# Modulation products with the condition rows stationary on four column groups

## The chip, the cores and the metric

One core of one Trainium2 chip runs one program. The time is that of the device for one execution, in microseconds (us), the median of several runs. TensorE (PE in the profile, with its weight loads as PEld), VectorE (DVE), ScalarE (ACT), GpSimd (POOL) and SyncE (SP) each work through a stream of instructions of their own and wait for each other through semaphores. SyncE, GpSimd and ScalarE also issue the transfers between memory and SBUF. In this kernel GpSimd does almost nothing else.

## The reference

One step of a two-layer decoder, for a prompt of 1,024 rows and eight sample sequences of four rows, 1,056 rows in all, model width 1,024, float32. The first layer is gated linear attention, the second differential attention, which reads keys and values made in between. Each of the three norms is modulated by a condition vector `c`, one for the prompt and one for each sample, nine rows:

```
def ada_mod(x, c, g, w_ada, b_ada, n):
    mod = jax.nn.silu(c) @ w_ada + b_ada
    parts = [p[:, None, :] for p in jnp.split(mod, n, axis=-1)]
    h = rms_norm(x, g) * (1.0 + parts[1]) + parts[0]
    return h, parts[2:]
```

`parts[2:]` are the gates on the output projections. Three weights are used, `ada_w_a` (1024 x 3072, first norm and first gate), `ada_w_kv` (1024 x 2048) and `ada_w_b` (1024 x 3072). In tiles of 128 columns, that is 24 + 16 + 24 = 64 tiles, each a product of a 1024 x 128 block with nine vectors.

## The kernel before

Everything is held transposed, the features on the partitions. The program has stages that end in a barrier: `setup`, `gla` (four heads), an output projection, `attention` (eight heads), an output projection. The tile `mod` (128 x 64 x 9) holds the modulation, a tile of 128 features in each of 64 places, `M_A` = 0, `M_KV` = 24, `M_B` = 40. `cT` holds silu(c), transposed.

`setup` turns x into `B2` (TensorE transposes, L281, VectorE copies, L367), stores it to memory (L336), makes the first norm (squares on ScalarE L136, sums on VectorE L143, a sum over partitions by `pe_sum` L148, `act_rstd`, then `dve_rstd` L161, which multiplies x in place and so waits for the store), and applies the modulation on ScalarE (`act_affine`, L169), with the low part of a high and low split on VectorE (L406). All 24 tiles of `ada_w_a` are made here, in three groups of four quarters: `cT` is stationary, 256 columns of the weights move (L301), into rows of nine partitions, which are copied (L384), turned (L309) and placed (L388). A fourth of a group is 1 MB; SyncE loads two of the four buffers and GpSimd two.

`gla` runs the same body for each head `i`. TensorE's order in a head is written out by hand: keys (units 3 to 5), the gate, z (units 9 to 14), the modulation products `modulate(0)` and `modulate(1)`, the value projection `project_v`, then a loop over eight chunks `t`, each with `levels(t + 1)` (L626), for t up to 4 another `project_v`, `output(t)` (L637, L639), for t = 1 to 6 one `modulate`, and `update(t + 1)` (L647). Behind the loop stand the products of the eight sample states (L701), `modulate(8)`, the update of the sample states (L708), `modulate(9)`, the next head's query projection and the sums of squares (L719). Each result goes to one of the two banks of `psP`; the n-th result of a head is `unit` n, counted in `s_proj` when summed and in `s_pfree` when copied out, so that a bank waits for the copy of the unit two before.

A modulation product (L649 to L654) makes one tile of 128: for each of eight `k`, the 128x128 block of weights is stationary and the nine columns of `cT[:, k, :]` move. ScalarE places it with the bias (L770). The 40 tiles of `ada_w_kv` and `ada_w_b` are made so, ten a head. GpSimd loads each tile's weights, 512 KB, into one of two buffers `wm` as soon as the product two before is done (L559).

In the chunk loop VectorE masks the eight level products (L921), reduces them (L926, into `Am`, which `output(t)` needs), and updates the state (L933); in chunk 5 it also makes the low part of the next head's first weights (L855), for which ScalarE must have made the high part (L740) behind the copy of that chunk's output (L826). The state of the samples, `sst`, 1 MB, has a tile of its own and is loaded by SyncE at the head's start (L516) and stored at its end (L520); behind that store stands the store of `Gs` (L526), for which VectorE waits at the end of the head (L957).

## Time and profile before

| | |
|---|---|
| runs | 1987.09, 1981.51, 1983.03 us; median 1983.03 |
| span of the profiled execution | 1985.5 us (its own time is not given apart) |
| TensorE busy | 1825.2 us (92%) |
| VectorE, ScalarE busy | 716.8 us (36%), 707.4 us (36%) |
| GpSimd busy | 234.2 us (12%), transfers issued |
| mean granted TensorE clock | 0.908 of 2.4 GHz |
| memory | 158.03 MB moved, mean 80 GB/s |

A busy share is an average over stages; what a stage is worth is read from that stage. An idle stretch of an engine is shown in brackets with what ended it. float32 products show as two records each. The granted clock is 1.00 or 0.50 in any short stretch, that is 2.4 or 1.2 GHz.

### The profile page before, as it was taken

To read this page: it belongs to the slowest core of one execution; us is meant where nothing else is said; L and a number is where in the kernel's file an instruction comes from. 1 tells how busy PE (TensorE), PEld (TensorE's weight loads), DVE (VectorE), ACT (ScalarE), POOL (GpSimd) and SP (SyncE) were. 2 spreads that over 40 slices of the span, in tenths; PEclk is the share of its full clock that TensorE was granted. 3 is DMA by queue.
4 is the path that set the end of the run, shared out by engine and by line. 5 is a ranking of instruction groups with operands and counts; after the bars stand their busy time and mean duration, and the time that the engine had idled before them with its cause. 6 is when DMAs were issued, how large, how long until landed. Compare 5 with 4: busy or idle time off the path is not lost. (4 is left out here: it accounts for less than half of the span.)

```text
span 1985.5 us, 32185 instructions
## 1 busy us (share of the span) xinstructions
PE 1825.2 (92%) x10195; PEld 1469.0 (74%) x10195; DVE 716.8 (36%) x1296; ACT 707.4 (36%) x1241; POOL 234.2 (12%) x372
## 2 busy tenths in 40 slices
PE   6899999999999969879998999989999899998798
PEld 3499889889889959746675776757767576665698
DVE  4536347327427533323215132141221412314321
ACT  2433143134125131254245343443434434344411
POOL 0011001100100100022030120311202112030000
PEclk8999799879878959989899898998999989999799
DMA  8622231231221242333022220222202222021143
GB/s 304 195 65 55 66 118 54 67 116 46 77 86 54 67 140 87 119 99 98 23 66 61 65 83 20 67 62 64 84 19 67 63 63 85 19 69 52 33 119 87
DMA packets 129119, 158.03 MB, mean 80 GB/s; under 512 B 13331, under 2 KB 103986, under 8 KB 129051
## 3 DMA queue, kind: packets, MB, share of 16 engines
q0 software_dynamic: 23776, 73.46, 12.6%
q1 hardware_dynamic: 94330, 70.61, 11.6%
q10 hardware_dynamic: 10944, 12.98, 1.9%
q8 instruction: 52, 0.85, 0.2%
q14 instruction: 17, 0.13, 0.0%
HBM read 127.41 MB, written 29.59 MB: 79 GB/s over the span
## 5 line engine op out<-in xcount | busy, mean ns | idle before, releaser
L1341 PE MATMUL at_psP<-B,w 128*128 128x352 f32 x768 | 253.4, 489 | 16.1 <-ACTq L1488 16.1
L1341 PEld LDWEIGHTS at_psP<-B,w 128*128 128x128 f32 x768 | 154.2, 203 | 102.6 <-issue 31.4
L1326 POOL DMA_DIRECT2D at_vc<-in_cache_v x256 | 139.0, 543 | 275.0 <-issue 275.0
L1065 PE MATMUL op_ps<-op_G_high,op_w_high 128*128 128x352 f32 x384 | 126.3, 329 | 30.4 <-DVE op_G_low L1135 25.6
L574 PE MATMUL gl_psP<-Hh,gl_w_high 128*128 128x352 f32 x384 | 131.9, 344 | 3.3 <-ACT gl_qT L757 1.7
L1350 PE MATMUL at_psP<-w,B 128*128 128x128 f32 (+1 forms) x1152 | 132.4, 275 | 0.0
L1350 PEld LDWEIGHTS at_psP<-w,B 128*128 128x128 f32 (+1 forms) x1152 | 129.6, 183 | 2.7
L574 PE MATMUL gl_psP<-Hl,gl_w_high 128*128 128x352 f32 x384 | 129.0, 336 | 0.0
L574 PE MATMUL gl_psP<-Hh,gl_w_low 128*128 128x352 f32 x384 | 128.5, 335 | 0.0
L1065 PE MATMUL op_ps<-op_G_low,op_w_high 128*128 128x352 f32 x384 | 124.5, 324 | 0.0
L1065 PE MATMUL op_ps<-op_G_high,op_w_low 128*128 128x352 f32 x384 | 124.5, 324 | 0.0
L1651 DVE CUSTOM_DVE_ANT_0 at_S<-at_psS,at_bias 128x256 f32<-128x256 f32 (+7 forms) x128 | 92.2, 754 | 79.2 <-PE at_psS L1377 78.8
L1341 PE MATMUL at_psP<-B,at_w_z 128*128 128x352 f32 x384 | 114.9, 459 | 0.0
L1395 PE MATMUL at_psO<-at_wT,at_v 128*128 128x128 f32 x576 | 83.9, 295 | 25.1 <-ACT G L1554 25.1
L1686 DVE SCALAR_TENSOR_TENSOR G<-G,at_subg,at_rs 128x1056 f32 x8 | 10.6, 1319 | 256.8 <-ACT at_rs L1600 256.8
L1341 PEld LDWEIGHTS at_psP<-B,at_w_z 128*128 128x128 f32 x384 | 73.0, 190 | 40.6
L1395 PEld LDWEIGHTS at_psO<-at_wT,at_v 128*128 128x128 f32 x576 | 76.5, 207 | 31.8 <-issue 29.2
L1065 PEld LDWEIGHTS op_ps<-op_G_high,op_w_high 128*128 128x128 f32 x384 | 73.4, 191 | 32.6 <-DVE op_G_low L1135 27.2
L1541 ACT ACTIVATE at_S<-at_S,at_nmx 128x256 f32<-128x256 f32 (+7 forms) x128 | 97.3, 763 | 0.0
L653 PEld LDWEIGHTS gl_psP<-cT,gl_wm 128*128 128x128 f32 x640 | 93.4, 232 | 2.9 <-issue 2.6
L653 PE MATMUL gl_psP<-cT,gl_wm 128*128 128x9 f32 x640 | 93.3, 284 | 0.0
L1377 PE MATMUL at_psS<-at_kT,at_qT 64*128 64x512 f32 (+3 forms) x384 | 85.4, 528 | 5.6 <-ACT at_ko L1534 5.4
(252 smaller groups left out, 3342.9 us busy)
## 6 DMA issues: line engine op xcount, KB each, us to landing
at_kc<-in_cache_k SPq DMA_DIRECT2D x256, 64.0 KB, 1.9
at_vc<-in_cache_v POOLq DMA_DIRECT2D x256, 64.0 KB, 2.2
w<-in_w_in_a POOLq DMA_DIRECT2D x24, 512.0 KB, 5.5
gl_wm<-in_ada_w_b POOLq DMA_DIRECT2D x24, 512.0 KB, 4.6
gl_wm<-in_ada_w_kv POOLq DMA_DIRECT2D x16, 512.0 KB, 6.0
su_w<-in_ada_w_a POOLq DMA_DIRECT2D x6, 1024.0 KB, 8.8
su_w<-in_ada_w_a SPq DMA_DIRECT2D x6, 1024.0 KB, 9.9
scr_xT<-B ACTq DMA_DIRECT2D x1, 4224.0 KB, 14.6
```

What stands on the lines that cost most here:

```text
L574: mm = nc.tensor.matmul(out, stationary(a, k), moving(b, k), start=(k == 0 and n == 0), stop=(k == KC - 1 and n == 2))
L653: mm = nc.tensor.matmul(psP[:, b, 0:NC], wm[:, n % MS, k, :], K["cT"][:, k, :], start=(k == 0), stop=(k == KC - 1))
L1065: mm = nc.tensor.matmul(ps[:, u % 2, 0:THIRD], ws[:, b, k, :], thirds(gs[:, k, :])[j], start=(k == 0 and n == 0), stop=(k == KC - 1 and n ...
L1326: pool.dma_start(vc[:, bass.ds(n, 1), :], A["cache_v"][bass.ds(page, 1), :, bass.ds(i, 1), :].rearrange("n p h d -> p (n h) d")).then_inc( ...
L1341: mm = nc.tensor.matmul(psP[:, unit % 2, 0:THIRD], w[name][:, k, :], thirds(src[:, k, :])[unit % 3], start=(k == 0), stop=(k == KC - 1))
L1350: mm = nc.tensor.matmul(psP[0:n, (9 + r) % 2, (t - lo) * P:(t - lo + 1) * P], hk[:, k, t * P:t * P + n], w["v"][:, k, :], start=(k == 0), ...
L1377: mm = nc.tensor.matmul(psS[:, 2 * comp + lo // 512, 0:hi - lo], qT[rows, t * P:(t + 1) * P], kT[rows, lo:hi], start=True, stop=True)
L1395: mm = nc.tensor.matmul(psO[:, (t % 2) * P:(t % 2 + 1) * P], v[:, k, :], wT[:, t % 2, k * P:(k + 1) * P], start=(k == 0), stop=(k == t))
L1541: A_(s, s, ACT.Exp, scale=-1.0, bias=nmx[:, t % 2, comp:comp + 1], accum_out=rsum[:, t % 2, comp:comp + 1]).then_inc(s_exp, 1)
L1651: V.tensor_tensor_reduce(S[:, t % 2, comp, 0:n], psS[:, 2 * comp:2 * comp + 2, :].rearrange("p a k -> p (a k)")[:, 0:n], bias[:, TP - n:TP ...
L1686: V.scalar_tensor_tensor(g, g, subg[:, 0:1], rs[:], ALU.mult, ALU.mult).then_inc(s_g1, 1)
```

## The change

The condition rows become the stationary operand everywhere, padded from nine to 32 columns with zeros (`CW`), and the weights move. The output is then 32 partitions high, and four such products stand in the four column groups of the array, each with its own quarter of the weight's columns (`CG` = 4).

In `setup` only the first 2,048 columns of `ada_w_a` are multiplied, which the first norm needs: eight loads of 128 rows x 2,048 columns (1 MB each, four buffers), for each one four multiplications of 512 columns. The sum for the norm comes after the fourth. The result, 128 partitions x 512, is copied, turned by four full transposes and placed. `xt` has five buffers instead of three, and the weight loads begin when the fifth x tile is there.

In `gla`, each head makes twelve tiles (48 in all, the rest of `ada_w_a` among them) in four products `modulate(0)` to `modulate(3)`. Each takes two blocks of 128 rows of a weight, 1,536 columns wide (`MW` = 384 in each column group), and VectorE adds them up in `macc` (`keep_mods`). In chunk 4 `turn_mods` turns the sum with three transposes and VectorE places it (`place_mods`). A load of both `wm` buffers waits for the product before. The two products ahead of the value projection stay where they were; two stand in chunks 1 and 2, and none behind that. ScalarE has no part in it any more. The count of freed banks is kept apart for each bank (`s_pf`). The sample state moves into rows of `B2` that the level products use, so its load waits for the last of them (`s_lv`), and VectorE waits for its store at the end of the head. GpSimd's loop over heads is unrolled.

```diff
+CG = 4
+CW = 32
...
+            K["cT"] = sb("cT", [P, KC, CW], c)
...
-        XB = 3
+        XB = 5
         xt = tile("xt", [P, XB, D])
-        mrow = tile("mrow", [NC, 2, 512])
-        w = tile("w", [P, 4, KC, 256])
+        mrow = tile("mrow", [P, 512])
+        w = tile("w", [P, 4, CG * 512])
...
-        def load_mod(eng, slots):
-
-            wd = A["ada_w_a"].rearrange("(k p) n -> p k n", p=P)
-            with eng.Fori(0, GROUPS) as i:
-                for j in slots:
-                    eng.wait_ge(s_wfree, i * 4 + j + 1)
-                    apart(eng, passed[slots[0]])
-                    eng.dma_start(w[:, j], wd[:, :, bass.ds(i * 1024 + 256 * j, 256)]).then_inc(s_w[j], 16)
-
-        passed = {0: K["sem"]("passed_sp"), 1: K["sem"]("passed_pool"), "pe": K["sem"]("passed_pe")}
+        def load_mod(eng, first):
+
+            for k in range(first, KC, 2):
+                if k >= 4:
+                    eng.wait_ge(s_wfree, k - 3)
+                else:
+                    eng.wait_ge(s_x[XB - 1], 16)
+                eng.dma_start(w[:, k % 4], A["ada_w_a"][k * P:(k + 1) * P, 0:CG * 512]).then_inc(s_w[k % 4], 16)
...
+                nc.gpsimd.memset(cT[:], 0.0).then_inc(s_set, 1)
+                load_mod(pool, 1)
...
-                def modulations(i):
-                    for j in range(4):
-                        pe.wait_ge(s_w[j], (i + 1) * 16)
-                        for k in range(KC):
-                            mm = nc.tensor.matmul(psM[0:NC, j // 2, (j % 2) * 256:(j % 2 + 1) * 256], cT[:, k, :], w[:, j, k, :],
-                                                  start=(k == 0), stop=(k == KC - 1))
-                        mm.then_inc(s_wfree, 1)
-                    for b in range(2):
-                        pe.wait_ge(s_mrow, 2 * i + b + 1)
-                        pe.wait_ge(s_mev, 2 * i + b + 1)
-                        apart(pe, passed["pe"])
-                        for m in range(4):
-                            mm = nc.tensor.transpose(psT[:, b, m * NC:(m + 1) * NC], mrow[:, b, m * P:(m + 1) * P], ident[0:NC, 0:NC])
-                        mm.then_inc(s_mT, 1)
-
-                modulations(0)
-                norm.pe_sum(pe)
-                with pe.Fori(1, GROUPS) as i:
-                    modulations(i)
+                for k in range(KC):
+                    pe.wait_ge(s_w[k % 4], 16 * (k // 4 + 1))
+                    for j in range(CG):
+                        mm = nc.tensor.matmul(psM[32 * j:32 * j + 32, 0, :], cT[:, k, :], w[:, k % 4, 512 * j:512 * (j + 1)], start=(k == 0), stop=(k == KC - 1))
+                    mm.then_inc(s_wfree, 1)
+                    if k == 3:
+                        norm.pe_sum(pe)
+                pe.wait_ge(s_mrow, 1)
+                for m in range(4):
+                    mm = nc.tensor.transpose(psT[:, 0, m * P:(m + 1) * P], mrow[:, m * P:(m + 1) * P], ident[:])
+                mm.then_inc(s_mT, 1)
...
-                dve.sem_inc(s_mev, 2)
-
-                def modulations(i):
-
-                    for b in range(2):
-                        dve.wait_ge(s_wfree, i * 4 + 2 * b + 6)
-                        nc.vector.tensor_copy(mrow[:, b, :], psM[0:NC, b, :]).then_inc(s_mrow, 1)
-                    for b in range(2):
-                        dve.wait_ge(s_mT, 2 * i + b + 1)
-                        at = i * 8 + 4 * b
-                        nc.vector.tensor_tensor(mod[:, bass.ds(at, 4), :], psT[:, b, 0:4 * NC].rearrange("p (m c) -> p m c", c=NC),
-                                                bcast(vec[:, bass.ds(at, 4)].unsqueeze(2), P, 4, NC), ALU.add).then_inc(s_mev, 1)
-
-                modulations(0)
                 dve.wait_ge(s_out, 16)
                 norm.dve_rstd(dve)
-                modulations(1)
-                dve.wait_ge(s_mev, 2 + 4)
+                dve.wait_ge(s_wfree, KC)
+                nc.vector.tensor_copy(mrow[:], psM[:, 0, :]).then_inc(s_mrow, 1)
+                dve.wait_ge(s_mT, 1)
+                nc.vector.tensor_tensor(mod[:, M_A:M_A + 16, :].rearrange("p (j m) c -> p j m c", j=CG),
+                                        psT[:, 0, :].rearrange("p (m j x) -> p j m x", j=CG, x=CW)[:, :, :, 0:NC],
+                                        bcast(vec[:, M_A:M_A + 16].rearrange("p (j m) -> p j m", j=CG).unsqueeze(3), P, CG, 4, NC), ALU.add).then_inc(s_mev, 1)
+                dve.wait_ge(s_mev, 1)
...
-    MODS, MS = 10, 2
+    MODS, MS, MW = 4, 2, 384
...
-        wm = tile("wm", [P, MS, KC, P])
-        sst = tile("sst", [P, SB, DV])
+        wm = tile("wm", [P, MS, CG * MW])
+        macc = tile("macc", [P, MW])
...
+        sst = X[:, 5:7, :].rearrange("p a t -> p (a t)")[:, 0:SB * DV].rearrange("p (b d) -> p b d", b=SB)
...
+        def freed(eng, i, unit):
+
+            eng.wait_ge(s_pf[unit % 2], i * (UNITS // 2) + (unit // 2 + 2))
...
-        V_UNITS = {(0, 2): 17, (2, 4): 18, (4, 5): 19, (5, 6): 20, (6, 7): 22, (7, 8): 24, (8, 9): 26}
-        M_UNITS = [15, 16, 21, 23, 25, 27, 28, 29, 30, 31]
-        M_CHUNK = [[], [2], [3], [4], [5], [6], [7], [], [8, 9]]
-        UNITS = 32
+        V_UNITS = {(0, 2): 17, (2, 4): 18, (4, 5): 19, (5, 6): 20, (6, 7): 22, (7, 8): 24, (8, 9): 25}
+        M_UNITS = [15, 16, 21, 23]
+        T_UNITS = [26, 27]
+        M_CHUNK = [[], [2], [3], [], [], [], [], [], []]
+        UNITS = 28
...
+                    sp.wait_ge(s_lv, CH * (i + 1))
+                    apart(sp, passed["sp"])
                     sp.dma_start(sst[:], A["state_gla"][:, bass.ds(i, 1), :, :].rearrange("b h k v -> k (b h) v")).then_inc(s_sin, 16)
...
+                    parts = [(wa, 2 * D, wkv, 0), (wkv, 512, wkv, 512 + D), (wb, 0, wb, D), (wb, D + 512, wb, 2 * D + 512)][i]
                     for n in range(MODS):
 
-                        pool.wait_ge(s_proj, i * UNITS + (UNITS + M_UNITS[n - MS] if n >= MS else M_UNITS[n - MS]) + 1)
-                        apart(pool, passed["pool"])
-                        src = wkv[:, :, bass.ds(i * 4 * P + n * P, P)] if n < 4 else wb[:, :, bass.ds(i * 6 * P + (n - 4) * P, P)]
-                        pool.dma_start(wm[:, n % MS], src).then_inc(s_wm[n % MS], 16)
-                        if n == 3 and not last:
+                        pool.wait_ge(s_proj, i * UNITS + (UNITS + M_UNITS[n - 1] if n else M_UNITS[MODS - 1]) + 1)
+                        for kk in range(MS):
+                            rows = slice((MS * n + kk) * P, (MS * n + kk + 1) * P)
+                            pool.dma_start(wm[:, kk, 0:D], parts[0][rows, parts[1]:parts[1] + D]).then_inc(s_wm[kk], 16)
+                            pool.dma_start(wm[:, kk, D:D + 512], parts[2][rows, parts[3]:parts[3] + 512]).then_inc(s_wm[kk], 16)
+                        if n == 1 and not last:
...
                     def modulate(n):
-                        pe.wait_ge(s_wm[n % MS], 16 * (MODS // MS * i + n // MS + 1))
                         b = bank(i, M_UNITS[n])
-                        for k in range(KC):
-                            mm = nc.tensor.matmul(psP[:, b, 0:NC], wm[:, n % MS, k, :], K["cT"][:, k, :], start=(k == 0), stop=(k == KC - 1))
+                        for kk in range(MS):
+                            pe.wait_ge(s_wm[kk], 32 * MODS * i + 32 * (n + 1))
+                            for j in range(CG):
+                                mm = nc.tensor.matmul(psP[32 * j:32 * j + 32, b, 0:MW], K["cT"][:, MS * n + kk, :], wm[:, kk, MW * j:MW * (j + 1)],
+                                                      start=(kk == 0), stop=(kk == MS - 1))
                         mm.then_inc(s_proj, 1)
+
+                    def turn_mods():
+                        freed(pe, i, M_UNITS[MODS - 1])
+                        for u, subs in zip(T_UNITS, ((0, 1), (2,))):
+                            b = bank(i, u)
+                            for m in subs:
+                                mm = nc.tensor.transpose(psP[:, b, (m % 2) * P:(m % 2 + 1) * P], macc[:, m * P:(m + 1) * P], ident[:])
+                            mm.then_inc(s_proj, 1)
...
                         output(t)
                         for n in M_CHUNK[t]:
                             modulate(n)
+                        if t == 4:
+                            turn_mods()
                         if t + 1 < NT:
...
-                    modulate(NT)
                     pe.wait_ge(s_khm, i + 1)
                     pe.wait_ge(s_lm, CH * i + CH)
                     for b in range(SB):
                         mm = nc.tensor.matmul(psL[:, b // 2, (b % 2) * DV:(b % 2 + 1) * DV], khm[:, b, :], v[0:TS, NT, :], start=True, stop=True)
                     mm.then_inc(s_ups, 1)
-                    modulate(NT + 1)
...
-                    def modulation(n):
-                        b = done(i, M_UNITS[n])
-                        apart(act, passed["act"])
-                        A_(mod[:, bass.ds(mod_tile(i, n), 1), :].rearrange("p a c -> p (a c)"), psP[:, b, 0:NC], ACT.Identity,
-                           bias=vec[:, bass.ds(mod_tile(i, n), 1)]).then_inc(s_pfree, 1)
+                        act.sem_inc(s_pf[b], 1)
...
+                    def keep_mods(n):
+
+                        unit = M_UNITS[n]
+                        dve.wait_ge(s_proj, (i + 1) * UNITS + unit + 1)
+                        if n:
+                            freed(dve, i, M_UNITS[n - 1])
+                            V.tensor_tensor(macc[:], macc[:], psP[:, unit % 2, 0:MW], ALU.add).then_inc(s_pf[unit % 2], 1)
+                        else:
+                            V.tensor_copy(macc[:], psP[:, unit % 2, 0:MW]).then_inc(s_pf[unit % 2], 1)
+
+                    def place_mods():
+
+                        tiles = bass.ds(i * M_HEAD + M_FIRST, M_HEAD)
+                        for u, lo, n in zip(T_UNITS, (0, 2), (2, 1)):
+                            dve.wait_ge(s_proj, (i + 1) * UNITS + u + 1)
+                            apart(dve, passed["dve"])
+                            V.tensor_tensor(mod[:, tiles, :].rearrange("p (j m) c -> p j m c", j=CG)[:, :, lo:lo + n, :],
+                                            psP[:, u % 2, 0:n * P].rearrange("p (m j x) -> p j m x", j=CG, x=CW)[:, :, :, 0:NC],
+                                            bcast(vec[:, tiles].rearrange("p (j m) -> p j m", j=CG)[:, :, lo:lo + n].unsqueeze(3), P, CG, n, NC),
+                                            ALU.add).then_inc(s_pf[u % 2], 1)
...
+                        if L >= 5:
+                            keep_mods(L - 5)
...
+                        if t in (1, 2):
+                            keep_mods(t + 1)
+                        if t == 4:
+                            place_mods()
...
+                    dve.wait_ge(s_sout, 16 * (i + 1))
```

## Rows read from the trace of the kernel before

**Rows 1.** The page's busy times: TensorE and its weight loads, the others.

```profile
PE 1825.2 (92%) x10195; PEld 1469.0 (74%) x10195; DVE 716.8 (36%) x1296; ACT 707.4 (36%) x1241; POOL 234.2 (12%) x372
```

**Rows 2.** Windows view, instructions on `gl_wm` alone: PE, PEld, POOL busy, PEclk, DMA share, GB/s.

```profile
100.00:720.00 620.00, 93.31 (x640) 93.37 (x640) 37.02 (x40) 0.87 0.25 73
```

**Rows 3.** Timeline of TensorE in head 1: start, length in us, instruction, idle before.

```profile
309.11 3.63 PE L653 MATMUL gl_psP<-cT,gl_wm 128*128 128x9 f32 x32
...
340.82 1.85 PE L653 MATMUL gl_psP<-cT,gl_wm 128*128 128x9 f32 x16
...
376.67 0.49 PE L637 MATMUL gl_psO<-gl_Am,gl_v 128*128 128x128 f32 x2 [3.60 <-DVE gl_Am L926]
...
377.82 3.42 PE L653 MATMUL gl_psP<-cT,gl_wm 128*128 128x9 f32 x16
...
382.69 0.80 PE L637 MATMUL gl_psO<-gl_Am,gl_v 128*128 128x128 f32 x2
...
385.46 1.92 PE L701 MATMUL gl_psO<-gl_ec,gl_sst 128*128 128x4 f32 x16 [0.85 <-ACT B L826]
...
391.66 3.58 PE L653 MATMUL gl_psP<-cT,gl_wm 128*128 128x9 f32 x16
```

**Rows 4.** Timeline of VectorE and GpSimd in head 1.

```profile
311.78 0.88 POOL L559 DMA_DIRECT2D gl_wm<-in_ada_w_kv  x1 [24.06 <-PE gl_psP L653]
...
313.70 1.32 DVE L900 TENSOR_TENSOR gl_gk<-B 128x1024 f32<-128x1024 f32 x2
...
325.23 1.26 DVE L916 TENSOR_TENSOR gl_gk<-gl_gk,gl_kT 128x1056 f32<-128x1056 f32 x1
...
372.36 1.23 DVE L855 TENSOR_TENSOR gl_w_low<-w,gl_w_high 128x1024 fp32r<-128x1024 f32 x1 [5.45 <-ACT gl_w_high L740]
373.50 1.22 DVE L921 TENSOR_TENSOR gl_tmp<-gl_psL,gl_masks 128x1024 f32<-128x1024 f32 x1
374.75 1.87 DVE L926 TENSOR_REDUCE gl_Am<-gl_tmp 128x128 f32<-128x1024 f32 x1
```

**Rows 5.** Windows: PE, PEld, DVE, ACT, POOL busy, PEclk, DMA share, GB/s.

```profile
32.00:67.00 35.00, 33.67 (x153) 14.43 (x154) 22.04 (x27) 13.45 (x13) 3.91 (x5) 0.95 0.98 336
...
312.70:316.00 3.30, 3.30 (x17) 3.30 (x17) 3.27 (x9) 3.01 (x4) 2.32 (x3) 0.50 0.73 176
...
377.50:384.30 6.80, 6.80 (x34) 6.08 (x34) 4.43 (x6) 0.65 (x2) 1.77 (x2) 0.50 0.11 12
...
387.70:411.60 23.90, 23.90 (x87) 21.82 (x87) 4.45 (x9) 3.61 (x5) 0.39 (x1) 0.50 0.14 46
```

**Rows 6.** Timeline of TensorE, an attention head: L1377 two row groups, L1408 full height.

```profile
1054.09 1.13 PE L1377 MATMUL at_psS<-at_kT,at_qT 64*128 64x512 f32 x4
...
1056.58 1.07 PE L1408 MATMUL at_psP<-at_ko,at_QZ 128*64 128x512 f32 x2
...
1073.37 2.04 PE L1377 MATMUL at_psS<-at_kT,at_qT 64*128 64x512 f32 x8
```

**Rows 7.** DMA issues: count, KB each, median us from issue to landing.

```profile
gl_wm<-in_ada_w_b POOLq DMA_DIRECT2D x24, 512.0 KB, 4.6
...
scr_xT<-B ACTq DMA_DIRECT2D x1, 4224.0 KB, 14.6
...
gl_sst<-in_state_gla SPq DMA_DIRECT2D x4, 1024.0 KB, 7.1
out_state_s<-gl_sst SPq DMA_DIRECT2D x4, 1024.0 KB, 4.4
```

**Rows 8.** Timeline of the setup: TensorE, VectorE, ScalarE.

```profile
50.93 14.08 PE L301 MATMUL su_psM<-su_w,cT 128*9 128x256 f32 x64
...
54.67 9.44 DVE L161 TENSOR_TENSOR B<-B,su_rs 128x1056 f32<-128x1056 f32 x8 [5.42 <-ACT su_rs L156]
...
66.79 1.24 ACT L169 ACTIVATE Hh<-B,mod 128x1024 fp32r<-128x1024 f32 x1 [12.22 <-DVE mod L397]
```

**Rows 9.** Timeline of TensorE at the end of head 3.

```profile
712.81 6.79 PE L719 MATMUL gl_psL<-B,ones 128*128 128x352 f32 x12 [2.29 <-ACT B L834]
```

More of the change, by code:

```diff
@@ L284, in _ @@
                         pe.wait_ge(s_tab, 16 * TABS)
-                        nc.tensor.transpose(psM[:, 0, 0:V_N], rows[:], ident[0:V_N, 0:V_N]).then_inc(s_vecT, 1)
+                        nc.tensor.transpose(psM[:, 0, 0:V_N], rows[:], ident[0:V_N, 0:V_N]).then_inc(s_turn, 1)
                         pe.wait_ge(s_csil, 1)
@@ L288, in _ @@
                             mm = nc.tensor.transpose(psM[:, 1, k * NC:(k + 1) * NC], crow[:, k * P:(k + 1) * P], ident[0:NC, 0:NC])
-                        mm.then_inc(s_cps, 1)
+                        mm.then_inc(s_turn, 1)
                 pe.wait_ge(s_lsum, 2)
                 pe.wait_ge(s_vec, 1)
-                nc.tensor.matmul(psM[:, 0, 0:2], ones[0:1, :], lams[0:1, :], start=True, stop=True).then_inc(s_lps, 1)
+                nc.tensor.matmul(psM[:, 0, 0:2], ones[0:1, :], lams[0:1, :], start=True, stop=True).then_inc(s_turn, 1)
                 pe.wait_ge(s_xev, 2 * (NT + 1))
@@ L406, in low @@
                     nc.vector.tensor_tensor(K["Hl"][:, k, :], xT[:, k, :], K["Hh"][:, k, :], ALU.subtract).then_inc(s_lo, 1)
-                for k in range(KC - 2):
-                    low(k)
-                modulations(2)
-                for k in range(KC - 2, KC):
+                for k in range(KC):
                     low(k)
 def gla(nc, A, OUT, SCR, K):
-    MODS, MS = 10, 2
+    MODS, MS, MW = 4, 2, 384
     with ExitStack() as c:
@@ L472, in gla @@
         s_lowps, s_low = sem("low_summed"), sem("low_ready")
-        s_proj, s_pfree = sem("proj_summed"), sem("proj_bank_free")
+        s_proj, s_pf = sem("proj_summed"), [sem(f"proj_bank_free{b}") for b in range(2)]
         s_v = sem("v_ready")
@@ L565, in _ @@
                 load_g2(0)
-                over_heads(pool, head)
+                for i in range(HA):
+                    head(i, i == HA - 1)
             @block.tensor
@@ L781, in head @@
                     for j in range(3):
-                        A_(thirds(kT[:])[j], psP[:, done(i, 3 + j), 0:THIRD], ACT.Copy).then_inc(s_pfree, 1)
+                        A_(thirds(kT[:])[j], psP[:, done(i, 3 + j), 0:THIRD], ACT.Copy).then_inc(s_pf[(3 + j) % 2], 1)
                     high(i, Z_TILE + 1, 5)
@@ L826, in head @@
                         A_(Gs[:, :, t * P:t * P + n], psO[:, 0:2 * n].rearrange("p (a t) -> p a t", a=2), ACT.Copy).then_inc(s_oev, 1)
-                        for m in M_CHUNK[t]:
-                            modulation(m)
                         if t == 5 and not last:
```

54 lines of the change are left out of this document (25 added, 29 removed).

## The prediction

> **What bounds the kernel now.** I began with the page's busy times [rows 1]: TensorE is busy 92% of the span, VectorE and ScalarE each about a third. So time on TensorE's own instruction stream is what counts, until a wait appears in it. Next the windows view of the instructions that touch the weight buffer `gl_wm` [rows 2]: the 40 modulation products of the four heads hold TensorE for 93.3 us, and the weight loads are in progress for as long. Each product is eight loads of a full 128x128 block for nine moving columns. Then the timeline of head 1 [rows 3], where the reader is to see three places. Two products stand back to back ahead of the value projection (3.63 us). Six stand in the loop over chunks, of which five take 1.85 us and the sixth, behind a 3.60 us idle, 3.42 us. Two stand in the tail, 3.58 us each (one row stands for both), with no idle between the sample products and the next head's query projection. The timeline of the other engines in the same head [rows 4] says what ends the 3.60 us idle: VectorE's reduction, which stood behind a weight split that waited for ScalarE. The windows by clock [rows 5] show that the short products are also where the clock is lost: 1.2 GHz (0.50) from 312.7 to 316.0 behind two of them, again from 377.5, and through the 23.9 us of the tail.
>
> **The new product.** Per head: four products instead of ten, each of eight multiplications of 384 moving columns, in four column groups. The old setup products give the serial price: 32 multiplications of 256 columns took 14.08 us [rows 8], 0.44 us each, so 0.66 us for 384 columns and 5.2 us for a product. Do the four column groups run at the same time? No row shows column groups. The nearest rows are the attention scores, which lie in two row groups [rows 6]: one full-height multiplication of 512 columns takes 1.07 us, two half-height ones 1.13 us, four 2.04 us. Two groups run at once, at no cost per group. If four column groups do the same, a product is two steps of 0.66 us and 0.2 us of drain, 1.5 us. Bounds: 1.5 and 5.2 us; I take 1.5, since the groups seen behave that way.
> The Trainium skill, page "TensorE: Matmul & The Clock Gate", section "Part 3: Packing small matmuls", gives a measured 2.38 times for three column tiles of 32 at 512 columns; by it, as an estimate, a product would cost 1.6 us. The same section says that a weight load overlaps matmuls in flight only where the row group differs, and here all four groups share their rows; by that the product would be serial or worse. The trace does not bear this out for full blocks: loads and products of one row group fill the same 93 us [rows 2].
>
> **Ahead of the value projection.** Before, products 0 and 1 each had their own buffer, loaded long ahead. Now one product uses both buffers (two blocks of 128 rows), and its load waits for the end of the product before. Products 0 and 1 are still back to back in TensorE's stream. So product 1 waits for a whole load: two blocks of 0.75 MB, four DMA issues on GpSimd's queue. An issue took 0.88 us for a transfer in 1,024 pieces [rows 4]; with 256 pieces I take 0.6. A 0.5 MB weight transfer lands 4.6 us after its issue [rows 7]. First block: 0.4 (release) + 0.6 + 4.4 = 5.4 us behind product 0; second about 1.8 us later; then its 0.75 us of product. The value projection starts at 309.1 + 1.5 + 7.2 + 0.75 = 318.5 instead of 312.6: +5.9 us (4 to 9). The idle costs clock too, where 3.3 us at half clock are paid already [rows 5]: +0.8. Queued behind product 1: the value projection on TensorE; on VectorE, the copy of product 1 stands before the k-hat differences and the level multiplications, 11.5 us from 313.70 to 325.23 [rows 4], which meet the 13.0 us of projection up to the first level product; they stay hidden by about 1 us. Together +6.7 us a head.
>
> **In the chunk loop.** Products 2 and 3 gain 0.35 us each; product 3's load has the 6.2 us between them, so 0.3 us of wait. Products 4 to 6 (old numbering) leave, 1.85 each, and three transposes come, 0.6 us. What this frees meets VectorE: it now waits in order for the products (0.5 us to add each) and for the transposes in chunk 4, before it may mask chunk 5. From the transposes on the chain is VectorE's: placing 0.5, mask and reduce 3.2 us [rows 4], against 2.3 us of update and levels on TensorE, so chunk 5's output waits 1.4 us. Then 0.9 us of output, 1.5 of ScalarE's copy and split, the low part 1.2, mask and reduce 3.2, chunk 6's output. In head 1's old times the transposes end at 362.9 and that output moves from 376.67 to about 373.3; chunk 7's, which had the 3.42 us product ahead, moves from 382.69 to 376.9, VectorE's state update, mask and reduce behind it.
>
> **The sample state.** It moves into rows that the levels use, so its 1 MB load is issued only when the last level product is done (375.8 in the same times: 373.3, 1.4 of output, 0.6 of update, 0.5), not half a head ahead. It took 7.1 us when it shared the engines with a store of G, which it no longer does; a 1 MB store alone took 4.4 [rows 7]. I take 5.7 with 0.3 for SyncE: the sample products start at 381.8 instead of 385.46, 3.7 us earlier, where without this wait they would start at 379.5. So 2.3 us of it is exposed. The wait for the state's store before the next head costs nothing: the store of G is issued behind it on the same queue, and VectorE waits for that already.
>
> **The tail.** Two products leave: -7.2 us. ScalarE no longer waits for them, so squares and sums follow sooner. The query projection behind runs at half clock now; with denser work ahead it may run at full, and against that the sample products stay at half longer. I take -1.0 (-3 to +1.5). Heads 0 to 2: 6.7 - 3.7 - 7.2 - 1.0 = -5.2 us each, -15.6. In head 3 there is no split in chunk 5 and no 3.60 us idle: its chunk loop gives back only about 0.3. But the sums wait for ScalarE's squares behind the last product until 712.81 [rows 9]; they then follow the last state update, 6.1 us sooner. Head 3: 6.7 - 0.3 - 6.1 = +0.3 us.
>
> **The setup.** The products shrink from 96 of 256 columns to 32 of 512, and the weights from 12 MB to 8. The end is set elsewhere: the x rows, squares, the sum over partitions, the scaling of 9.44 us from 54.67, then ScalarE's affine from 66.79 [rows 8]. Five x tiles now come first, the weights behind them, and the small tables share the engines with less, so I take x as turned some 4 us sooner (1 to 6). The sum no longer waits for products, but the scaling waits for the store of x to memory, 4.3 MB, which took 14.6 us with little beside it [rows 7]. Now 4.2 MB of weights go beside it: both at the 336 GB/s of this stretch [rows 5] are 25 us, from about 27.8 to 53, so the scaling starts at 53 instead of 54.67. The copy, four transposes and the addition stand behind it, 2 us, where before 2.7 us did. I take -3 us (-8 to +1).
>
> **Sum.** -15.6 + 0.3 - 3 = -18.3 us against the profiled execution. The page gives only its span, 1985.5 us, which lies 2.5 above the median of the runs; I take what lies around it as unchanged and subtract from the median: 1983.0 - 18.3 = 1964.7, 1965 us.
>
> **Rivals.** *Serial column groups* (ends on the other side). A product costs 5.2 us: product 0 and 1 add 6.4 more a head, products 2 and 3 7.4 more; VectorE's slack gives back some 2. About +11.8 a head on the forecast, +47 in all; in the setup the store hides it: 2012 us. Place: every product in the heads. It decides from about 2.9 us a product on, where the total crosses zero. For it: no row has column groups. Against: [rows 6]. By the Trainium skill's rule on loads, quoted above, it would be this case. *The waits cost clock.* Each head gets two idles that it did not have, 5 and 2 us, and the row behind the 3.60 us idle is 6.8 us of half clock [rows 5]. If each idle brings as much, the value projection loses 3 us more than now and the tail gains nothing: some +3.5 a head, 1979 us. *Cheaper all round*: the loads land in 4 us and the query projection runs at full clock: -3 a head more, the setup -8: 1948 us. *The change does not do what it says* has no place here: the instructions are fixed.
>
> **Chances.** Forecast 0.60 (own range 1950 to 1972), clock 0.17, serial 0.15, cheaper 0.08. Range: down to 1944 for the cheap case; upward it takes in the clock case with the upper load bound, 1990, and leaves out the serial one. A measurement of this kernel tells 0.3%, 6 us, from no change. Faster: forecast, cheap and a third of the clock case, 0.73; same: 0.11; slower: serial and a tail, 0.16.
>
> **What would show it.** In the profile after: the products' line near 4 x 1.5 us a head and four starts a few tens of ns apart (serial: 0.66 us apart); an idle of about 5 us inside product 1, ended by a DMA into `gl_wm`; 1 to 2 us of idle before the sample products ended by the DMA into the state; chunk 5's output waiting for VectorE; the affine at about 64 us. The prediction is wrong if product 1's idle is over 9 us, if VectorE's levels end after the value projection, or if half clock spreads into the projections.

## The result and the profile after

The changed kernel takes 1989.35 us (median of 5 runs, 1988.21 to 1990.97); beside it the kernel before took 1983.03 us (1981.51 to 1987.09). The ratio is 1.0032, 95% interval 1.0019 to 1.0045: about 0.3% slower, where 1965 us was predicted. The time lies just inside the range, by its upper end.

The profiled executions hide the difference: spans of 1985.5 and 1986.4 us. A further trace of each (runs below) explains that. Executions lie some 2 us above their spans, so the profiled one of before took 1987.09 us, its slowest run; the second trace of that kernel has a span of 1978.4 us, the second of the changed kernel 1991.6 us. So stages are compared here as means of two traces each. By these the work behind the four heads begins at 732.6 us before and at 739.6 us after, and the rest is equal. The loss of 7.0 us is all in setup and heads.

The page's busy times of the changed kernel (compare [rows 1]), then the windows view of the instructions on `gl_wm` ([rows 2]; PE, PEld, POOL, clock, DMA share, GB/s):

```profile
PE 1739.4 (88%) x9675; PEld 1374.7 (69%) x9675; DVE 720.1 (36%) x1310; ACT 696.9 (35%) x1201; POOL 229.1 (12%) x395
```

```profile
100.00:720.00 620.00, 30.85 (x256) 6.22 (x256) 35.46 (x64) 0.87 0.25 80
```

TensorE lost 86 us of busy time, 62 of them in the head products, and the kernel gained nothing: idle time stands in the place of the work. The waits of TensorE in the heads say which (total us, times, longest; a wait of 21.1 us ahead of head 0 is left out):

```profile
PE gl_psO L627 <- DVE gl_Am L942: 20.0, 11, 3.6
PE gl_psP L644 <- DMA gl_wm<-in_ada_w_kv: 16.8, 6, 7.9
PE gl_psO L703 <- DMA B<-in_state_gla: 15.1, 4, 4.6
PE gl_psP L644 <- DMA gl_wm<-in_ada_w_b: 12.4, 5, 5.2
```

Three of the four rows are transfers, 44.3 us, and no such row stands among the waits of the kernel before. Its row for the reduction into `gl_Am` is the first one's counterpart, and that has grown by 9.2 us, in chunk 5 above all:

```profile
PE gl_psO L637 <- DVE gl_Am L926: 10.8, 3, 3.6
```

The timeline of TensorE in head 1 shows their places (compare [rows 3]):

```profile
311.54 1.50 PE L644 MATMUL gl_psP<-gl_wm,cT 128*32 128x384 f32 x16
320.94 1.50 PE L644 MATMUL gl_psP<-gl_wm,cT 128*32 128x384 f32 x8 [7.90 <-DMA gl_wm<-in_ada_w_kv]
323.00 1.51 PE L644 MATMUL gl_psP<-gl_wm,cT 128*32 128x384 f32 x8 [0.56 <-DMA gl_wm<-in_ada_w_kv]
...
362.49 0.85 PE L644 MATMUL gl_psP<-gl_wm,cT 128*32 128x384 f32 x8 [0.80 <-DMA gl_wm<-in_ada_w_kv]
...
379.71 0.49 PE L627 MATMUL gl_psO<-gl_Am,gl_v 128*128 128x128 f32 x2 [1.77 <-DVE gl_Am L942]
...
386.68 0.61 PE L627 MATMUL gl_psO<-gl_Am,gl_v 128*128 128x128 f32 x2 [3.59 <-DVE gl_Am L942]
...
395.98 3.54 PE L703 MATMUL gl_psO<-gl_ec,B 128*128 128x4 f32 x16 [4.61 <-DMA B<-in_state_gla]
...
400.01 3.58 PE L703 MATMUL gl_psO<-gl_ec,B 128*128 128x4 f32 x16
```

Product 0 takes 1.50 us. Product 1 waits 7.90 us for its first block, and then each half takes 1.5 us. A half of product 3, at full clock, takes 0.85 us, and the window of product 1 below shows the clock at half. The windows by clock (columns as in [rows 5]):

```profile
320.00:324.40 4.40, 2.91 (x16) 0.40 (x16) 0.00 (x0) 1.12 (x2) 0.00 (x0) 0.50 0.90 291
...
396.00:420.00 24.00, 24.00 (x89) 20.65 (x90) 4.36 (x9) 4.88 (x5) 0.89 (x1) 0.62 0.19 55
```

GpSimd issues that load the moment product 0 ends at 313.0, four transfers for the two blocks (compare the issue of 0.88 us in [rows 4]):

```profile
313.36 0.53 POOL L546 DMA_DIRECT2D gl_wm<-in_ada_w_kv  x1 [23.01 <-PE gl_psP L644]
314.19 0.54 POOL L547 DMA_DIRECT2D gl_wm<-in_ada_w_kv  x1 [0.29 <-issue]
...
315.25 0.54 POOL L547 DMA_DIRECT2D gl_wm<-in_ada_w_kv  x1
```

In the setup, rows of TensorE, VectorE and ScalarE, and the DMA issues of that stretch (compare [rows 7, 8]):

```profile
26.00 4.56 PE L281 MATMUL su_psT<-ident,su_xt 128*128 128x128 f32 x20 [1.79 <-DMA su_xt<-in_x_prompt]
```

```profile
58.25 9.44 DVE L163 TENSOR_TENSOR B<-B,su_rs 128x1056 f32<-128x1056 f32 x8 [14.49 <-DMA scr_xT<-B]
```

```profile
70.11 1.24 ACT L171 ACTIVATE Hh<-B,mod 128x1024 fp32r<-128x1024 f32 x1 [18.84 <-DVE mod L381]
```

```profile
scr_xT<-B ACTq DMA_DIRECT2D x1, 4224.0 KB, 26.4
su_xt<-in_x_prompt ACTq DMA_DIRECT2D x8, 512.0 KB, 7.3
su_w<-in_ada_w_a SPq DMA_DIRECT2D x4, 1024.0 KB, 10.7
su_w<-in_ada_w_a POOLq DMA_DIRECT2D x4, 1024.0 KB, 13.5
```

The scaling began 3.6 us later than before, the affine 3.3 us. What released the scaling is a store: x, turned, goes to memory, and that took 26.4 us in place of 14.6.

### The profile page after: what moved, and what is told of

The parts are those of the page before. It is cut to its first block and busy times, and to the rows that moved or that the text cites. A ratio compares the mean times of both kernels' runs of the same rounds, so it can differ in the third digit from the quotient of the medians.

```text
span 1986.4 us, 30767 instructions
## 1 busy us (share of the span) xinstructions
PE 1739.4 (88%) x9675; PEld 1374.7 (69%) x9675; DVE 720.1 (36%) x1310; ACT 696.9 (35%) x1201; POOL 229.1 (12%) x395
## 5 line engine op out<-in xcount | busy, mean ns | idle before, releaser
L1086 PE MATMUL op_ps<-op_G_high,op_w_high 128*128 128x352 f32 x384 | 127.4, 332 | 29.7 <-DVE op_G_low L1156 25.7
L1672 DVE CUSTOM_DVE_ANT_0 at_S<-at_psS,at_bias 128x256 f32<-128x256 f32 (+7 forms) x128 | 92.2, 753 | 77.9 <-PE at_psS L1398 77.7
L1362 PE MATMUL at_psP<-B,at_w_z 128*128 128x352 f32 x384 | 114.9, 459 | 0.0
L1416 PEld LDWEIGHTS at_psO<-at_wT,at_v 128*128 128x128 f32 x576 | 74.4, 202 | 31.8 <-issue 29.2
L564 PE MATMUL gl_psP<-gl_w_high,Hh 128*128 128x256 f32 (+1 forms) x288 | 86.0, 299 | 0.0
L564 PE MATMUL gl_psP<-gl_w_low,Hh 128*128 128x256 f32 (+1 forms) x288 | 83.8, 291 | 0.0
## 6 DMA issues: line engine op xcount, KB each, us to landing
scr_xT<-B ACTq DMA_DIRECT2D x1, 4224.0 KB, 26.4
```

The lines of the kernel that those rows point to most:

```text
L564: mm = nc.tensor.matmul(out, stationary(a, k), moving(b, k), start=(k == 0 and n == 0), stop=(k == KC - 1 and n == 2))
L1086: mm = nc.tensor.matmul(ps[:, u % 2, 0:THIRD], ws[:, b, k, :], thirds(gs[:, k, :])[j], start=(k == 0 and n == 0), stop=(k == KC - 1 and n ...
L1362: mm = nc.tensor.matmul(psP[:, unit % 2, 0:THIRD], w[name][:, k, :], thirds(src[:, k, :])[unit % 3], start=(k == 0), stop=(k == KC - 1))
L1416: mm = nc.tensor.matmul(psO[:, (t % 2) * P:(t % 2 + 1) * P], v[:, k, :], wT[:, t % 2, k * P:(k + 1) * P], start=(k == 0), stop=(k == t))
L1672: V.tensor_tensor_reduce(S[:, t % 2, comp, 0:n], psS[:, 2 * comp:2 * comp + 2, :].rearrange("p a k -> p (a k)")[:, 0:n], bias[:, TP - n:TP ...
```

## The experiments

All ratios are to the kernel before on the same chip. Its medians there were 1985.86 us (runs 1 to 4), 1986.65 (runs 5 to 7) and 1985.31 (runs 8 and 9). A ratio is the one on record, which can differ by some 0.1% from that of the two medians.

**1. The kernel before again**, one execution.

> The kernel before, unchanged, once more with a profile, because its profiled execution was the slowest of its runs (1987.09 us) and the median is 1983.0. If the difference between executions lies in the granted clock, the four heads together differ by 2 to 5 us between the two profiles, stage by stage only where half-clock stretches lie, and the setup is the same to 0.5 us (affine from 66.8). If it lies in transfers, the waits for them differ instead.

1980.07 us, span 1978.4 us, 7.1 us under the first trace. Its heads 0 to 3 take 155.0, 156.1, 150.9 and 113.3 us, against 156.2, 156.4, 155.1 and 114.9, at a mean granted clock of 0.912 against 0.908. That is 7.3 us in the heads, more than the 2 to 5 expected; the setup agrees to 0.5 us, as expected. One trace of this kernel doesn't place a difference of 0.3%.

**2. Product 1 later.** It goes behind the first two parts of the value projection, with its sum on VectorE moved along (`keep_mods(1)` and the unit numbers; those lines are left out here).

```
...
-        M_UNITS = [15, 16, 21, 23]
+        M_UNITS = [15, 18, 21, 23]
...
                     modulate(0)
-                    modulate(1)
...
                     project_v(2, 4)
+                    modulate(1)
```

> Product 1 of each head moves behind the value projection of chunks 0 to 3, so that its load has 14 us of projection beside it; its place in VectorE's stream moves with it. Theory A (the heads give back their gain in product 1's wait for its own load): the stretch from the end of z to the first level product falls from 22.0 to 26.3 us per head to 16 to 17 us, the 29 us of idle ended by the weight transfers fall to under 3, and the time falls by 25 to 33 us, to about 1960. Theory B (the wait is covered, VectorE's level work would be the bound in its place): the stretch ends later than 19 us and the time falls by under 12 us. Theory C (the clock takes it back): the waits go but half-clock stretches grow elsewhere in the head by as much, and the time falls by under 15 us.

1960.09 us, ratio 0.9868 (0.985 to 0.9885). TensorE in head 1 of this run:

```profile
304.16 1.50 PE L644 MATMUL gl_psP<-gl_wm,cT 128*32 128x384 f32 x16
307.49 0.38 PE L564 MATMUL gl_psP<-gl_w_high,Hh 128*128 128x256 f32 x1 [1.84 <-DVE gl_w_low L847]
...
319.10 1.50 PE L644 MATMUL gl_psP<-gl_wm,cT 128*32 128x384 f32 x16
```

Product 1 waits for nothing and takes 1.50 us again. From product 0 to the value projection it is now 3.3 us in heads 0 to 2, against 11.5 in the changed kernel, and the window from 306 to 330 us, which ran at a clock of 0.72 in the changed kernel, runs at 1.00. The projection now waits 1.84 us for VectorE's split of its weights, which the product used to cover. The sample state is still waited for, 4.5 to 4.8 us in heads 0 to 2. This one order is worth more than the whole loss, and all of the forecast for it (theory A) came true.

**3. The sample state early.** It gets a tile of its own, loaded at the head's start; the sum of the products (`macc`) goes to the rows of `X` instead. With it VectorE's two additions for products 0 and 1 move behind the k-hat differences (those lines are left out here).

```
-        macc = tile("macc", [P, MW])
+        sst = tile("sst", [P, SB, DV])
...
+        macc = X[:, NL, 0:MW]
...
-                    sp.wait_ge(s_lv, CH * (i + 1))
-                    apart(sp, passed["sp"])
```

> The sample state has a tile of its own again and is loaded at the head's start; to make room the sum of the products lies in the row of the running sums, and both of VectorE's additions for products 0 and 1 stand behind the k-hat differences. Product 1's wait stays. Theory A (the late load of the state costs its idle): the idle before the sample products falls from 4.3, 4.6, 3.5 and 2.7 us to 0.9 or less, and the time falls by 8 to 13 us. Rival: that idle only stands in for a wait on ScalarE and VectorE that ends as late, then the time falls by under 4 us.

1972.83 us, ratio 0.9938 (0.992 to 0.9956). The sample products of head 0 and of head 1, each with its line from TensorE's timeline:

```profile
235.43 1.92 PE L701 MATMUL gl_psO<-gl_ec,gl_sst 128*128 128x4 f32 x16 [0.85 <-ACT B L818]
...
237.61 3.27 PE L701 MATMUL gl_psO<-gl_ec,gl_sst 128*128 128x4 f32 x16
```

```profile
385.33 3.54 PE L701 MATMUL gl_psO<-gl_ec,gl_sst 128*128 128x4 f32 x16 [0.85 <-ACT B L818]
```

The wait of 4.3 and 4.6 us in these two heads is down to the 0.85 us that the kernel before had [rows 3]. Head 0's first pass is back at 1.92 us; head 1's stays at 3.54. So the wait for the state isn't the only thing that puts this stretch at half clock. Up to the sample products the heads 0 to 2 take 67.5 us behind the start of the value projection, against 70.9 in the changed kernel, and 3.3 us of that is the wait; the moved additions are not seen. The whole gain, 0.9% or some 18 us, is above the 8 to 13 us expected.

**4. One column group.** All four quarters of a product go to partitions 0 to 31, one after the other.

```
-                                mm = nc.tensor.matmul(psP[32 * j:32 * j + 32, b, 0:MW], K["cT"][:, MS * n + kk, :], wm[:, kk, MW * j:MW * (j + 1)],
-                                                      start=(kk == 0), stop=(kk == MS - 1))
+                                mm = nc.tensor.matmul(psP[0:32, b, 0:MW], K["cT"][:, MS * n + kk, :], wm[:, kk, MW * j:MW * (j + 1)],
+                                                      start=(kk == 0 and j == 0), stop=(kk == MS - 1 and j == CG - 1))
```

The four quarters are added up in one place, so this kernel leaves out three of the four results; VectorE's additions take the same columns on 32 partitions (those lines are left out here).

> In the heads all four quarters of a product go to the first column group, one after the other into the same 32 partitions (so the modulation of the second norms, the keys' norm and the gates is wrong); loads, waits and orders are those of the changed kernel. The column groups' concurrency is worth what this loses. Theory A (four groups run at once, a product of 8 multiplications takes 1.50 us, serial ones 0.64 us each): a product takes 5.1 to 5.2 us, and the time rises by 40 to 50 us, to about 2034. Rival (the waits for loads hide it, since the two blocks of a product land 1 to 2 us apart): product 1 hides part, the time rises by 25 to 35 us.

2043.60 us, ratio 1.029 (1.0268 to 1.0311). TensorE in head 0:

```profile
156.83 5.35 PE L644 MATMUL gl_psP<-gl_wm,cT 128*32 128x384 f32 x16
...
168.38 7.93 PE L644 MATMUL gl_psP<-gl_wm,cT 128*32 128x384 f32 x16 [6.20 <-DMA gl_wm<-in_ada_w_kv]
```

The same eight multiplications take 5.35 us in one group and 1.50 us in four, a factor of 3.6. The time is 2.6% above the changed kernel's, some 52 us, where 40 to 50 were expected.

**5 and 6. The setup's transfers.** In run 5 the second four weight tiles wait for the store of the turned x. In run 6 the first four also wait for the last tile of x (the second edit below is run 6's alone).

```
                 if k >= 4:
                     eng.wait_ge(s_wfree, k - 3)
+                    eng.wait_ge(s_out, 16)
                 else:
-                    eng.wait_ge(s_x[XB - 1], 16)
+                    eng.wait_ge(s_x[NT % XB], 32)
```

> The changed kernel, with one edit in the setup: of the 4 MB of modulation weights, the second four tiles wait until the store of the turned x has landed. In the changed kernel that store landed 26.4 us after its issue (14.6 us in the kernel before), the norm's factor waited 14.5 us for it, and head 0 began 3.3 us later than before. Theory A (the store shares the DMA engines with weights that the added products want early): the store lands in 15 to 18 us, the affine is done at about 67 us in place of 70.1, head 0 begins near 87.5, and the time falls by about 3 us. Rival 1 (the late setup comes from the added products and the sums over the partitions, which wait 6.5 us for VectorE): the store lands early but the affine stays near 70, no change of the time. Rival 2: the deferred weights are now last; the affine moves to 73 or later and the time rises by 3 us or more.

> As the run with the store first, and the first four weight tiles also wait, for the last tile of x to land, in place of the fourth last. TensorE waited 2.1 and 1.8 us for tiles of x in the changed kernel. Theory A: x is turned by 27 to 29 us in place of 31.4, the store is out of the way earlier, and the affine is done at 63 to 66 us: 4 to 7 us faster than the changed kernel. Rival: the transfers total the same bytes (some 17 MB before the first affine can be done), so that what x gains the weights lose; the affine lands where it does with the store first, within 1 us.

Run 5: 1981.16 us, ratio 0.9981 (0.9964 to 0.9998). Run 6: 1979.59 us, 0.9972 (0.9957 to 0.9986). The two can't be told apart. Both beat the changed kernel, though on another chip: their intervals end at 0.9998 and 0.9986, and its two begin at 1.0011 and 1.0019. Run 5's DMA issues, VectorE and ScalarE, then run 6's:

```profile
scr_xT<-B ACTq DMA_DIRECT2D x1, 4224.0 KB, 13.8
```

```profile
51.75 9.44 DVE L163 TENSOR_TENSOR B<-B,su_rs 128x1056 f32<-128x1056 f32 x8 [7.65 <-ACT su_rs L158]
```

```profile
63.15 1.24 ACT L171 ACTIVATE Hh<-B,mod 128x1024 fp32r<-128x1024 f32 x1 [11.53 <-DVE mod L382]
```

```profile
su_xt<-in_x_prompt ACTq DMA_DIRECT2D x8, 512.0 KB, 5.2
```

```profile
45.19 9.44 DVE L163 TENSOR_TENSOR B<-B,su_rs 128x1056 f32<-128x1056 f32 x8 [7.19 <-ACT su_rs L158]
```

```profile
61.47 1.24 ACT L171 ACTIVATE Hh<-B,mod 128x1024 fp32r<-128x1024 f32 x1 [16.41 <-DVE mod L382]
```

With the store undisturbed, the scaling waits for the norm's factor instead, and the affine comes 7.0 us earlier, not the 3 that I expected (and the time falls by 0.5%, some 9 us, not 3): I had taken the kernel before's affine, which waited for its own products, as the floor. Run 6 brings x down 6 us sooner (the last of it turned at 25.7 us), but then TensorE waits 8.8 us for the fifth weight tile and the affine gains only 1.7 us more. Both rivals, that the added products or the deferred weights set the end, fall for run 5. For run 6 the rival, that the weights lose what x gains, holds for most of the 6 us.

**7. Edits 2 and 3 together.**

> Both edits that were tried alone, in the changed kernel: the second product of each head behind the value projection's first two parts (alone 29 us faster than the changed kernel), and the sample state in a tile of its own, loaded at the head's start (alone 13 to 16 us faster). Theory A (two separate waits in series on TensorE): the gains add up, -42 to -45 us against the changed kernel, 1945 to 1948 us. Rival (the waits share a cause, the DMA queue of the head, so that one edit takes most of the other's gain): 1958 us or above. The sample products start within 0.5 us of the last score of the head and the idle time before them is under 1 us in each head.

1945.32 us, ratio 0.9788 (0.9773 to 0.9802). Against the changed kernel at 1.0028 (the mean of its two ratios), edit 2 alone gives 1.6%, edit 3 alone 0.9%, both 2.4%: the gains nearly add up, and the rival at 1958 us falls. The idle before the sample products is 0.6 to 0.9 us in each head.

**8. All three**, with the setup of run 6.

> The changed kernel with the three edits that each gave time: the second product behind the value projection's first two parts, the sample state in a tile of its own from the head's start, and x ahead of the weights in the setup (head 0 began 8.6 us earlier there). Theory A (three separate waits): 1945.3 less 8.6, 1936 to 1938 us, ratio to the kernel before 0.974 to 0.975. Rival (an earlier setup is given back in head 0, whose own transfers then wait for TensorE): 1943 us or above.

1937.41 us, ratio 0.9771 (0.9755 to 0.9787). Head 0 begins at 83.0 us, 7.5 earlier than in the changed kernel. The median lies in the range expected, 1936 to 1938 us, but the ratio lies above the 0.974 to 0.975 expected. The interval overlaps that of run 7, so the setup's share isn't shown by the ratios; the medians differ by 7.9 us on different chips. TensorE's waits in the heads:

```profile
PE gl_psO L626 <- DVE gl_Am L942: 19.3, 10, 3.6
...
PE gl_psP L563 <- DVE gl_w_low L846: 7.2, 4, 1.8
...
PE gl_psO L702 <- ACT B L819: 2.6, 3, 0.9
...
PE gl_psP L643 <- DMA gl_wm<-in_ada_w_kv: 1.4, 2, 0.8
```

Of the transfers only one is left among them, 1.4 us; the row for the sample state is gone. This version is 2.3% faster than the kernel before and 2.5% faster than the changed one.

**9. The changed kernel again.**

> The changed kernel unaltered, so that the small differences of the setup runs stand beside it on one chip: 1.002 to 1.0045 of the kernel before if the first measurement was right; its setup, its waits of the second product (5 to 8 us a head) and of the sample state (3 to 5 us a head) as in the first trace. If it comes out below 1.0 of the kernel before, the verdict of a slowdown was scatter between chips.

1990.56 us, ratio 1.0024 (1.0011 to 1.0038), within the 1.002 to 1.0045 expected. The slowdown is there on a second chip, with the same waits: 6.0 to 8.4 us inside product 1 and 3.1 to 4.6 us for the state.

## Why the prediction was wrong

The account, us per head for heads 0 to 2 and in total, from two traces of each kernel (a head is cut at its product 0, at the start of the value projection, at the sample products, and at the end of the sample state's update; differences are taken before rounding):

| part | before | after | measured | predicted |
|---|---|---|---|---|
| product 0 to value projection | 3.7 | 11.5 | +7.8 | |
| to the sample products | 73.3 | 70.9 | -2.4 | |
| sample products and update | 17.5 | 15.2 | -2.3 | |
| to the next product 0 | 60.4 | 58.1 | -2.3 | |
| product 0 to sample products | 77.0 | 82.4 | +5.4 | +6.7 - 3.7 = +3.0 |
| tail (sample products to the next product 0) | 77.9 | 73.3 | -4.6 | -7.2 - 1.0 = -8.2 |
| heads 0 to 2 together | 464.8 | 467.1 | +2.3 | -15.6 |
| head 3 | 114.1 | 115.9 | +1.9 | +0.3 |
| setup (to head 0) | 87.5 | 90.5 | +3.0 | -3 |

The sum is +7.2 against the -18.3 predicted (the 7.0 us above, with 0.1 us less from head 0's first projection to its product 0). Of the 25.5 us between them 10.8 lie in the tail, 7.1 between product 0 and the sample products, 6.0 in the setup and 1.6 in head 3. That the time still fell inside the range, by 0.65 us, is owed to the range's width: the rival "the waits cost clock" and an upper bound of its load carried it to 1990. The direction was wrong.

**The new product: right.** 1.50 us at full clock, as taken; serial it costs 5.35, the other bound was 5.2. The Trainium skill's figure for three column tiles ("TensorE: Matmul & The Clock Gate", "Part 3: Packing small matmuls") gave 1.6 as an estimate. The Trainium skill's rule in the same section is that a weight load overlaps multiplications in flight only where the row group differs, and it would have made this 2012 us or more. The trace doesn't agree for these four column groups: in head 1 four weight loads start at 311.89 us and four at 312.21, inside a product that runs from 311.54 to 313.04. The rival "serial" is refuted by the factor of 3.6 in run 4, whose 2043.6 us is even above the 2012 worked out for it.

**Ahead of the value projection: the wait right, its clock too small.** The idles ahead of and inside product 1 were 6.7, 8.5, 6.0 and 5.4 us in the four heads, 6.6 in the mean, where the sum had 6.45. But product 1 itself then ran at half clock in all four heads: 3.0 us for 1.5. I had put the clock's price at 0.8 us, by a row with less idle. From product 0 to the first level product it came to +7.6, not +6.7. What the prediction didn't ask was whether the product had to stand there at all. Run 2 shows it: nothing needs product 1 at that place, and the kernel gets 1.6% back.

**In the chunk loop and the sample state: mechanism right, size too large.** Chunk 5's output waits for VectorE, 1.77 us against 1.4. The state's load took 5.6 us from its issue to the sample products (head 0), as taken. But the chain ran later: with 324.44 - 312.59 = 11.85 us taken off, the shift of head 1's value projection, chunk 6's output of head 1 starts at 374.8, not 373.3, and chunk 7's at 378.3, not 376.9. So the sample products came 2.2 us sooner instead of 3.7, and what the load exposed was 3.3 to 4.6 us of wait in heads 0 to 2, 3.3 more than before in the mean, where I had 2.3. Run 3 shows its worth with the clock: 0.9% of the kernel.

**The tail: the step that failed.** The two products left, 7.2 us, as the rows say. I took 1.0 us of clock on top, expecting denser work to run faster. The opposite came: the sample products, 5.6 to 5.7 us together in two of the heads 0 to 2 of either trace before, took 7.6 us in every one, and from the update's end to the next product 0 only 2.3 us of the second product's 3.6 came back. The projection behind did not get its full clock sooner either: with the product taken off, it ran at half for 3.8 us before and 4.6 after, in the mean of heads 0 to 2. 3.6 us a head, 10.8 in all, is the largest error of the sum.

That the clock took back the part in the sample products is seen in the rows (3.54 us for 1.92). Where it fell can be read for the changed kernel. In head 1 it was back at full between chunk 7's output and the sample products, and fell while TensorE waited for the state (windows, columns as above):

```profile
390.50:393.50 3.00, 0.86 (x8) 0.67 (x7) 1.57 (x3) 0.38 (x1) 0.00 (x0) 1.00 0.71 188
394.00:396.00 2.00, 0.02 (x1) 0.05 (x1) 0.00 (x0) 0.00 (x0) 0.00 (x0) 0.50 0.63 211
```

Head 0 shows the same, but in head 2 the clock was at half before that wait already. And without the wait half clock came from elsewhere: in run 3 head 0 got 1.92 us and heads 1 and 2 got 3.54, and run 7 has 3.54 in heads 0 to 2 with an idle of 0.85 us. There a stretch of half clock that began in the idle of 3.6 us ahead of chunk 6's output, or behind it, was still running (in head 1 of run 3 from 377.9 us on, in head 1 of run 7 from 366.9). The kernel before has the same idle, but a product of 3.4 us stood behind it, and in head 1 its half clock ended at 384.3 us, just ahead of the sample products. That the product which left had given the clock time to come back is an argument and not shown: I didn't try other work ahead of the sample products.

**Head 3.** Product 1's place cost 4.6 us (I had 6.7), but the tail gave back only 2.6, not 6.1. The chunk loop gave next to nothing, as predicted. The tail's 6.1 us were for the sums of squares. I let them follow the last state update on TensorE; they write the bank that VectorE's update of the state has to read first. VectorE and TensorE in head 3 of the changed kernel:

```profile
711.96 3.22 DVE L966 SCALAR_TENSOR_TENSOR B<-B,gl_dec,gl_psL 128x256 f32<-128x256 f32 x8 [16.96 <-PE gl_psL L709]
```

```profile
715.33 6.80 PE L719 MATMUL gl_psL<-B,ones 128*128 128x352 f32 x12 [3.41 <-DVE B L966]
```

Before, the tail product covered this wait, and the releaser of [rows 9] hid it. When one wait was removed, the next one in the same place was missed.

**The setup: one assumed start.** "I take x as turned some 4 us sooner" failed: x was turned at 31.4 us, as before. The tiles of x, first in the order of issue, landed in 7.3 us each instead of 5.5, because the weights were issued beside them (5.2 us in run 6, where the weights wait for x). The next step was right in kind and nearly in size: the store beside the weights took 26.4 us, 25 were worked out, but it began at 31.8 us and not at 27.8, so the scaling did not begin at 53 but at 58.25, and the affine not at 64 but at 70.11. Run 5 removes the sharing with the second half of the weights, and head 0 begins at 83.6 us, 3.9 us before the 87.5 of the kernel before. That is the gain predicted, by another way than the one I gave: x is turned no sooner there, but the store lands in 13.8 us and the smaller products no longer hold the norm. So what the change saves there is real, and the order of the transfers took it back.

**The reference time.** I subtracted from the median of the runs a sum made against the profiled execution, whose span lay 2.5 us above that median. The sum should have been tied to several executions, since one trace of this kernel is up to 7 us from another. It explains none of the 25.5 us, which are differences of traces.

**The rival that came nearest** is "the waits cost clock", 1979 us with a chance of 0.17. It is a part of the cause: in product 1 and in the tail. The mean granted clock says the same: 0.895 to 0.904 in the thirteen runs of the changed kernel against 0.906 to 0.913 in those of the kernel before on record, and 0.905 to 0.911 again in run 2. The rest is transfers that had no cover: product 1's load, which the sum had nearly right, and the sample state and the store of x, which it had too small or too early. Of the three signs of being wrong that I named, the first did not come (product 1's idle, 8.5 us at most), and VectorE's levels held TensorE up once, by 0.3 us; the third, half clock in the projections, came only as the 0.8 us of the tail.

## What to carry to other kernels

When work shrinks to a third, its loads don't. Write down for every use of a buffer when its load can first be issued and what TensorE does between that moment and the use; two uses of one buffer back to back leave the whole landing time bare. Here one product moved behind two parts of the projection was worth 1.6%, more than five times the loss. Where a stall is removed, look for the next releaser in the same place (here the bank that VectorE still reads). And a transfer that leaves the critical path can still slow the one that is on it: order the setup's transfers by who is waited for first.

## What the runs showed of the hardware

Four column groups of 32 columns run four fp32 multiplications of 384 columns at once: 1.50 us for eight, 5.35 us in one group. The same product behind an idle of 5.1 to 7.9 us takes 3.0 us, at a granted clock of 0.50. The tail's eight multiplications of 4 columns take 1.92 us at a granted clock of 1.00 and 3.54 us at 0.50. A store of 4.3 MB took 13.8 us (run 5), 14.6 (before), 18.9 (run 6) or 26.4 us (the changed kernel), by what else was under way. Two profiled executions of the kernel before had spans of 1978.4 and 1985.5 us.
